# Expert stage: three of a group's eight diagonal matrices move from ScalarE to GpSimd

## The reference, cut to what matters

```
def block_fn(hb):                                   # 128 tokens, 1024 wide
    scores = ...                                    # 8 heads x 2 x 128 keys
    ...                                             # top 16 of 256 pairs per head
    idx  = ...reshape(tb, 8 * 16)                   # 128 experts for each token
    gate = softmax(best).reshape(tb, 8 * 16)
    u = take(expert_u, idx)                         # (tokens, 128, 1024)
    act = gelu(einsum("tkd,td->tk", u, hb))
    vv = take(expert_v, idx)                        # (tokens, 128, 1024)
    return einsum("tk,tkd->td", gate * act, vv)
x = rms_norm(x + out, final_norm_g)
```

## Time and profile before

| | |
|---|---|
| median of 3 runs | 2869.43 us |
| the profiled execution | 2876.21 us, its span 2874.8 us |
| mean granted TensorE clock | 0.934 |
| expert stage, first gather to the last | 2103.0 to 2844.1 us |
| busy in the span: TensorE, VectorE, ScalarE, GpSimd | 90%, 54%, 33%, 28% |
| bytes from GpSimd's queue | 268.47 MB of 557.35 |

### The profile page before, as it was taken

The page is one execution under the profiler, slowest core; times in us unless marked ns, Lnnn a source line. Parts: engine busy times, 40 slices in busy tenths (PEclk is TensorE's granted clock), DMA queues, the critical chain, the costliest instruction groups (busy, mean ns, idle before and its releaser), DMA issues.

```text
span 2874.8 us, 37721 instructions
## 1 busy us (share of the span) xinstructions
PE 2594.0 (90%) x15650; PEld 2150.2 (75%) x15650; DVE 1558.1 (54%) x3013; ACT 955.5 (33%) x1526; POOL 812.8 (28%) x668
## 2 busy tenths in 40 slices
PE   7999999998999999999989999998979776777777
PEld 7998998988999999998979978886865232233232
DVE  5446894425445447975334444245166655666552
ACT  4344544414344445544324421532012211211121
POOL 0005770000000016840000000000045666666663
PEclk9999999999999999999999999998989887888888
DMA  6565772034544555751035544440578999999996
GB/s 195 191 171 114 188 174 88 1 121 132 191 162 143 183 159 129 186 155 60 16 105 191 183 137 135 132 132 30 161 286 321 360 368 367 368 371 372 368 360 250
DMA packets 324731, 557.35 MB, mean 194 GB/s; under 512 B 16200, under 2 KB 245586, under 8 KB 324562
## 3 DMA queue, kind: packets, MB, share of 16 engines
q1 hardware_dynamic: 250834, 286.48, 33.6%
q0 software_dynamic: 73728, 268.47, 24.4%
HBM read 553.85 MB, written 1.05 MB: 193 GB/s over the span
## 4 chain that ended last, share of the span: by engine, by line
PE 72%; DVE 15%; issue 6%; another core or an unknown queue 2%; POOL 2%; ACT 2%; DMA 1%; SPq 0%; DVEq 0%; POOLq 0%
PE bank L333 15%; PE bank L2335 9%; PE bank L393 8%; PE bank L394 8%; PE bank L395 8%; PE banks_to L393 3%; PE banks_to L394 3%; PE banks_to L395 3%; DVE banks_to L917 3%; DVE proj L2284 2%; PE banks_to L1096 2%; PE banks_to L333 2%; DVE gdn_conv L1002 2%; PE bank L1096 2%
## 5 line engine op out<-in xcount | busy, mean ns | idle before, releaser
L393 PE MATMUL bank<-operand_hi,weights_high 128*128 128x256 f32 x2432 | 692.0, 285 | 24.4 <-DVE cnv_dw_cols L578 15.7
L394 PE MATMUL bank<-operand_lo,weights_high 128*128 128x256 f32 x2432 | 688.5, 283 | 0.0
L395 PE MATMUL bank<-operand_hi,weights_low 128*128 128x256 f32 x2432 | 683.6, 281 | 0.0
L393 PEld LDWEIGHTS bank<-operand_hi,weights_high 128*128 128x128 f32 x2432 | 462.4, 190 | 28.0 <-DVE cnv_dw_cols L578 16.1
L395 PEld LDWEIGHTS bank<-operand_hi,weights_low 128*128 128x128 f32 x2432 | 466.2, 192 | 0.0
L394 PEld LDWEIGHTS bank<-operand_lo,weights_high 128*128 128x128 f32 x2432 | 463.4, 191 | 0.1
L373 POOL TENSOR_TENSOR weights_low<-weights,weights_high 128x1024 fp32r<-128x1024 f32 x128 | 308.7, 2454 | 491.8 <-ACT weights_high L343 491.6
L343 ACT CAST weights_high<-weights 128x1024 fp32r<-128x1024 f32 x392 | 386.0, 1046 | 0.0
L387 DVE TENSOR_TENSOR weights_low<-weights,weights_high 128x1024 fp32r<-128x1024 f32 x264 | 308.0, 1221 | 128.9 <-ACT weights_high L343 128.9
L2335 PE MATMUL bank<-weights,residual 128*128 128x512 f32 x480 | 248.6, 658 | 88.8 <-issue 88.1
L2335 PE MATMUL bank<-proj,residual 128*128 128x512 f32 x484 | 246.3, 653 | 73.3 <-issue 73.2
(11 more groups left out here) (412 smaller groups left out, 3778.8 us busy)
## 6 DMA issues: line engine op xcount, KB each, us to landing
weights<-in_ffn_w_in SPq DMA_DIRECT2D x88, 1024.0 KB, 5.1
weights<-in_mix_w_in SPq DMA_DIRECT2D x64, 1024.0 KB, 11.1
weights<-in_ffn_w_out SPq DMA_DIRECT2D x44, 1024.0 KB, 4.9
weights<-in_w_in SPq DMA_DIRECT2D x24, 1024.0 KB, 5.4
weights<-in_cnv_w_o SPq DMA_DIRECT2D x8, 1024.0 KB, 6.4
weights<-in_gdn_w_o SPq DMA_DIRECT2D x8, 1024.0 KB, 5.2
weights<-in_mix_w_out SPq DMA_DIRECT2D x8, 1024.0 KB, 5.3
weights<-in_peer_w_q SPq DMA_DIRECT2D x8, 1024.0 KB, 5.4
```

Source lines behind the costliest of these rows:

```text
L393: t.matmul(out, w_hi, x_hi, start=start, stop=False, skip_group_check=skip)
L394: t.matmul(out, w_hi, x_lo, start=False, stop=False, skip_group_check=skip)
L395: return t.matmul(out, w_lo, x_hi, start=False, stop=stop, skip_group_check=skip)
```

## The change

From group 2 on, ScalarE makes only the diagonals 0 to 4 of a group. GpSimd makes the diagonals 5, 6 and 7, as a TENSOR_TENSOR product of the identity and the broadcast column of weights: diagonal 5 right behind the gather of v(i,3), 6 behind v(i,5), 7 behind v(i,7). Each waits for the weights of group i and for TensorE's last row of group i-2. They are counted by a semaphore of their own; TensorE, and the weights two groups later, wait for the one or the other. Groups 0 and 1 stay as they were. Order and number of the gathers, the dots and the matmuls are the same.

```diff
--- before.py
+++ after.py
@@ -23,6 +23,8 @@
 SLOTS, BANKS, HIGHS, AHEAD = 6, 3, 4, 2
 GROUP, U_ROWS, V_ROWS = 8, 12, 17
 HEADS, TOP, KEYS = 8, 16, 128
+
+POOL_DIAGONAL, DIAGONAL_BEHIND = 5, {3: 5, 5: 6, 7: 7}
 
 
 class Signal:
@@ -106,6 +108,7 @@
         self.v_in = [s(f"v_row_in{i}", 16) for i in range(V_ROWS)]
         self.dotted, self.gelu, self.weighed, self.diag, self.summed_v, self.taken = (
             s(n) for n in ("u_dotted", "expert_gelu", "expert_weighed", "diagonals", "expert_sum", "expert_sum_added"))
+        self.diag_pool = s("diagonals_by_pool")
         self.last_act, self.last_dve = s("last_norm_act"), s("last_norm_dve")
 
 
@@ -2260,7 +2263,7 @@
     return divmod(r, GROUP)
 
 
-def pool_rows(X, m, S, K, i, homes, landed, freed, table):
+def pool_rows(X, m, S, K, i, homes, landed, freed, table, diagonals=False):
 
     n, p = divmod(i, 2)
     X.pool.wait_ge(*S.choose.at(n, "chosen"))
@@ -2273,6 +2276,8 @@
             X.pool.wait_ge(*S.used.at(block))
         at = bass.IndirectOffsetOnAxis(ap=K.index[n % 3][:, p * GROUP + s:p * GROUP + s + 1], axis=0)
         landed[r % len(homes)].by(X.gpsimd.indirect_dma_start(out=home, out_offset=None, in_=table, in_offset=at), r)
+        if diagonals and i >= 2 and s in DIAGONAL_BEHIND:
+            pool_diagonal(X, m, S, K, i, DIAGONAL_BEHIND[s])
 
 
 def vector_dot(X, m, S, K, i, s):
@@ -2290,7 +2295,8 @@
     X.dve.wait_ge(*S.gelu.at(i))
     X.dve.wait_ge(*S.choose.at(n, "gate"))
     if i >= 2:
-        X.dve.wait_ge(*S.diag.at(i - 2, GROUP - 1))
+        X.dve.wait_ge(*S.diag.at(i - 2, scalar_diagonal_count(i - 2) - 1))
+        X.dve.wait_ge(*diagonal_at(S, i - 2, GROUP - 1))
     S.weighed.by(X.vector.tensor_tensor(K.weights[p], K.acts[p], K.gate[n % 3][:, p * GROUP:(p + 1) * GROUP], ALU.mult), i)
 
 
@@ -2312,13 +2318,29 @@
     S.gelu.by(X.scalar.activation(K.acts[i % 2], K.dots[i % 2], ACT.Gelu), i)
 
 
+def scalar_diagonal_count(i):
+
+    return POOL_DIAGONAL if i >= 2 else GROUP
+
+
 def scalar_diagonals(X, m, S, K, i):
     p = i % 2
     X.act.wait_ge(*S.weighed.at(i))
     if i >= 2:
         X.act.wait_ge(*S.summed_v.at(i - 2, GROUP - 1))
-    for s in range(GROUP):
+    for s in range(scalar_diagonal_count(i)):
         S.diag.by(X.scalar.activation(K.diag[p][:, s, :], m.ident[:, :], ACT.Copy, scale=K.weights[p][:, s:s + 1]), i, s)
+
+
+def pool_diagonal(X, m, S, K, i, s):
+    p = i % 2
+    X.pool.wait_ge(*S.weighed.at(i))
+    X.pool.wait_ge(*S.summed_v.at(i - 2, GROUP - 1))
+    S.diag_pool.by(X.gpsimd.tensor_tensor(K.diag[p][:, s, :], m.ident[:, :], K.weights[p][:, s:s + 1].to_broadcast([P, P]), ALU.mult), i, s)
+
+
+def diagonal_at(S, i, s):
+    return (S.diag if s < scalar_diagonal_count(i) else S.diag_pool).at(i, s)
 
 
 def tensor_group(X, m, S, K, i):
@@ -2329,7 +2351,7 @@
         X.bank_free(2 * half + 1)
     for s in range(GROUP):
         r = i * GROUP + s
-        w.wait_ge(*S.diag.at(i, s))
+        w.wait_ge(*diagonal_at(S, i, s))
         w.wait_ge(*S.v_in[r % len(K.v)].at(r))
         for c in range(2):
             ins = t.matmul(m.bank[2 * half + c][:, :], K.diag[p][:, s, :], K.v[r % len(K.v)][0][:, c * 512:c * 512 + 512],
@@ -2347,7 +2369,7 @@
         if i < GROUPS:
             pool_rows(X, m, S, K, i, K.u, S.u_in, S.dotted, io["peer_u_2"][0])
         if i:
-            pool_rows(X, m, S, K, i - 1, K.v, S.v_in, S.summed_v, io["peer_v_2"][0])
+            pool_rows(X, m, S, K, i - 1, K.v, S.v_in, S.summed_v, io["peer_v_2"][0], diagonals=True)
 
 
 HALF_DONE = HALF + 2
```

## The result

The changed kernel takes 2924.44 us (median of 4 runs, 2923.1 to 2928.98), the kernel before beside it 2869.25 us: a ratio of 1.0193, 95% interval 1.0178 to 1.0208. It is 55 us slower, where 25 us less were forecast, and lies above the range. The granted clock, 0.934 in both profiled executions, is not the cause.

A forecast was written before the change was run, and what follows sets the result against it. GpSimd's gather stream was taken to pace the expert stage: 635.2 + 49.5 + 20.2 + 21.4 = 726.3 us, 14.8 less; with 10 of tail, -24.8 from 2876.2 gives 2851.4, less 6.8 for the median: 2844.6 us. Range 2823 to 2919.

The forecast's parts named there:

- What bounds the stage: Expert stage, 741.1 us: GpSimd's gather stream paces it, 511 distances of 1.243 us (635.2 us) plus 105.9 us of stalls.
- the later stalls: GpSimd's stalls after 2186 us, 85.7 us, taken as a result of the saturated queue; a quarter, 21.4 us, was to stay.
- The removal from ScalarE: 90 diagonal activations leave ScalarE in the expert stage, 27.5 us of its work; costed at nothing.
- The product: 90 128x128 products added to GpSimd's gather chain at 0.55 us each: 49.5 us, ends 26 and 89 us.
- the sign of being right: Distance of GpSimd's gathers across one product: expected 1.79 us, forecast right if 1.63 to 2.23 us.
- What the pauses give back: Products' pauses let the DMA queue run dry, so most starved stretches go; 21.4 of 85.7 us of stalls stay.
- the second rival: No change: the expert stage needs a certain idle queue time, pauses only replace stalls; 2869 us, give or take 5; chance 0.15.
- Late weights cost nothing where starvation goes: GpSimd's wait behind v(i,3) for VectorE's weights: nothing where starved stretches go, 0 to 27.5 us (five groups) where they stay.
- the early stalls: GpSimd's five stalls up to 2186 us, waits for TensorE and the first rows; 20.2 us, kept in the forecast.
- The tail: After the last gather, TensorE would no longer end a group behind; 10 us of some 13 taken as gain.
- The first, starvation stays: Expert stage: all 85.7 us of stalls and the tail stay, products add in full; 2918.9 us; chance 0.32.
- The small rival beside it: Expert stage: starved stretches stay and late weights hold GpSimd in addition; up to 2946 us; chance 0.05.

The follow-up runs named there:

- e17: Kernel before plus a 128-column product of constants on GpSimd behind rows 0, 2, 4, 6 of each group from group 2 on (240 products); ratio 0.9981.
- e18: Kernel before plus a 128-column product of constants on GpSimd behind every gather from group 2 on (480 products); ratio 1.0216.
- e4: Changed kernel with group i's products behind gathers u(i+2,1), u(i+2,3), u(i+2,5), except the last two groups; 2871.55 us, ratio 1.0002.
- e2: Kernel before plus the 90 products at the change's places, from constants into scratch, ScalarE making all diagonals; 2870.71 us, ratio 0.9996.
- e1: Kernel before plus only the change's GpSimd waits behind v(i,3), no products, ScalarE making all diagonals; 2925.92 us, ratio 1.0199.
- e13: Kernel before plus a one-column GpSimd memset behind every gather from group 2 on, where the kernel before takes 2865.33 us; ratio 1.0008.
- e15: Changed kernel with GpSimd making diagonals in even groups only (45 products), where the kernel before takes 2865.33 us; ratio 1.0004.
- e3: Changed kernel with all three products of a group behind gather v(i,7), four gathers later; 2886.33 us, ratio 1.0052.
- e14: Changed kernel with VectorE making group i-1's weights before the first dot of group i, not behind the second; 2873.46 us, ratio 1.0027.
- e16: The changed kernel itself, run again on another chip where the kernel before takes 2867.88 us; ratio 1.0135.
- e10_before: The kernel before, unchanged, traced on a chip where it takes 2789.24 us.

## Why the prediction was wrong, point by point

**What bounds the stage: right as to GpSimd's stream, incomplete as to its stalls.** All kernels on the chips that starve have a stage of 511 x 1.243 us and something over it. That the later stalls come from the saturated queue held too: e17, feeding at 372 GB/s, and e18, at 334, lose them. Two readings were a little off: eight of the last ten slices of the earlier trace rows move 360 to 372 GB/s, not nine, and the 26 later stalls of over 0.5 us add up to 82.7 us; the other 3 us of the 85.7 are smaller delays.

**The removal from ScalarE: right.** It is worth nothing (e4 has it, at 1.0002).

**The product: mis-sized.** 0.33 us in the chain instead of 0.55, so 30 us instead of 49.5. That is below the 0.39 us that I called its lower end, and near the floor of 0.29; gathers across a product stand 1.53 us apart in e2, outside the 1.63 to 2.23 that I had named as the sign of being right. The instruction itself is as costed (0.41 us against 0.39). It is cheaper in the chain since it starts at once behind the gather and shares the gap of 0.30 us with the next.

**What the pauses give back: the step that failed first.** I let 64.3 of the 85.7 us go beyond what the products cost. e2 shows that 30 us of products gave back 27, e17 that 79 us gave back as much: nothing on top. This is what the second rival says of the products, and e18, which goes beyond its 86 us, pays for what lies beyond. The row that I leaned on, a free stretch of 17.3 us after a stall of 2.72 us, showed that a pause frees the engines for a while, not that three short ones do with less. The Trainium skill (DMA: Bandwidth & Descriptors, section "Where 436 GB/s comes from") names about 358 GB/s, half of a stack's 716, as a core's limit on the HBM side. This core's runs on chips B and C don't agree with it as a firm limit: 409 or 410 GB/s for 557 us. On the others the mean is near it (361 in the earlier trace rows, 367 to 370 from 2190 us on), though stretches of 20 us reach 409; the runs don't show the reason.

**Late weights cost nothing where starvation goes: the step that turned a zero into a loss.** I measured starvation by TensorE's matmuls. By that measure it went ahead of the hold shown above (28 matmuls in 14.7 us at 409 GB/s, against 10 in 20.2 us in the earlier trace rows), but not everywhere:

```profile
2283.00:2294.90 11.90, 4.38 (x6) 0.95 (x4) 2.26 (x7) 0.00 (x0) 8.85 (x11) 0.66 1.02 407
```

And the weights are made by VectorE, which stayed starved in the steps of its choice (224 us of waits, against 149). I had seen five groups in which the weights of before come too late and priced them at 27.5 us at most; there are eleven odd groups and three others, 112.1 us of idle time ahead of products. The first of the two halves was covered, as I wrote (a hold drains the queue as the stall does); the second wasn't: a stall ends when the queue is empty, a hold only when VectorE has then made up three dots. The cover that I named hid the draining and not the work behind it, 58.9 us of an empty queue.

**The sum.** Forecast for the stage: 635.2 + 49.5 + 20.2 + 21.4 = 726.3. Measured: 635.2 + 30 + 21.5 + 113.8 = 800.5. The products give 19.5 less, the early stalls 1.3 more, and the later stalls 92.4 more. The 92.4 have two parts. By that rival's rule, one us of stalls for one of products, 85.7 - 30 = 55.7 us of later stalls would be left, 34.3 above the forecast of 21.4; the other 58.1 are what the holds add, and the queue is empty for 58.9. With products and stalls in balance and no holds, the stage would have stayed near 742 us (an estimate by that rule). The tail gave 6.5 us of the 10 that I took, and the stage started 6.1 us earlier. The latter is not the change's: it starts between 2096.9 and 2098.1 in e1, e4, e13 and e15 as well, and between 2102.7 and 2103.5 in e2, e3, e14 and e18.

**The rivals.** The first, starvation stays, gave 2918.9 us, near the measured time by accident: its mechanism, products on top of unchanged stalls, is refuted by e2 and e17. The small rival beside it, late weights that hold GpSimd in addition, is the one that happened; it had 0.05 and too small a price. The second gives the right time for the products alone (e2), and for the whole change where the wait stands where it never bites (e4). That the chips differ was on no list.

**What stays open.** Why the engines beside a full queue starve on some chips and not on others; what else ran on those chips is not on record, and no run tests it. That the steps which wait are those in which an engine waits for its own last result is seen in the timelines, but no run takes those waits away. Nor is it shown why VectorE is less late in e16 than in the first run of the change, or why its waits add up to more in the kernels with the moved diagonals (221 us in e4 too, at no cost) than in the kernel before.

## What to carry to other kernels

A wait put on an engine that feeds others must be dated against the latest release in the trace, group by group, and its price here was the time for which the queue then stood empty: the work that the late engine still had to do once it ran again. Here short extra work on an engine that stalls was free up to the sum of its stalls and gave nothing back, on the chips that starve; and whether a stretch is starved must be read on the engine that is waited for. Move the wait rather than the work: here the same products cost 55 us behind v(i,3), 15 us behind v(i,7) and nothing another two to six gathers on.

## What the runs showed of the hardware

- The same kernel takes 2865 to 2871 us on some chips and 2789 us on others. The difference is the expert stage (741.1 against 646.2 us); the traffic is the same, and on the second kind GpSimd's gathers run at 409 to 410 GB/s for 557 us with all engines going freely beside them.
- Between two gathers of 512 KB on GpSimd (0.94 us and a gap of 0.30) a memset of 0.12 us adds nothing, and a product of 128 columns, 0.41 us, adds 0.33.
- On the first kind of chip, with the queue full (409 GB/s), many of VectorE's small dependent steps wait 2 to 6 us each; in e10_before no such step has a wait in its list from 2100 to 2740 us.
